# Inverting the 16x16 diagonal blocks on GpSimd ahead of TensorE's levels in the delta-rule inverse

## The reference, cut to what matters

```python
A = jnp.where(strict, jnp.einsum('nbhid,nbhjd->nbhij', kb, k) * decay, 0.0)
M = A + jnp.eye(L, dtype=A.dtype)
u = lax.linalg.triangular_solve(M, v * beta[..., None], left_side=True, lower=True, unit_diagonal=True)
w = lax.linalg.triangular_solve(M, kb * jnp.exp(G)[..., None], left_side=True, lower=True, unit_diagonal=True)
...
def step(S, inp):
    q_i, w_i, u_i, k_i, a_i, gl_i = inp
    v_new = u_i - jnp.einsum('bhld,bhde->bhle', w_i, S)
    o = jnp.einsum('bhld,bhde->bhle', q_i, S) + jnp.einsum('bhls,bhse->bhle', a_i, v_new)
```

## Time and profile before

| what | us |
|---|---|
| median of three runs | 1905.28 |
| the profiled execution | 1905.35 |
| its span, first to last instruction | 1903.5 |
| TensorE busy | 1857.1 |
| VectorE busy | 1354.1 |
| ScalarE busy | 959.2 |
| GpSimd busy | 110.8 |
| start to end of the inverse, first layer (L1352 to L1382) | 1035.39 to 1072.15 |
| start to end of the inverse, second layer | 1632.05 to 1668.81 |

### The profile page before, as it was taken

One profiled execution on the slowest core, in us unless ns is written; L12 is line 12 of the kernel. 1 busy time (PEld: TensorE's weight loads), 2 busy tenths in 40 slices (PEclk: granted clock), 3 DMA queues, 4 the chain that ended last, 5 costly groups with the idle time before them and its releaser, 6 DMA issues.

```text
span 1903.5 us, 31636 instructions
## 1 busy us (share of the span) xinstructions
PE 1857.1 (98%) x12720; PEld 1705.4 (90%) x12720; DVE 1354.1 (71%) x2154; ACT 959.2 (50%) x1429; POOL 110.8 (6%) x112
## 2 busy tenths in 40 slices
PE   8999999999999999999999999999999999999998
PEld 6888999888899989998988989998999888989997
DVE  5576788747677886777777777677766776875545
ACT  5666444656644454435655353435443665454343
POOL 0000000000000000000002201100110001400100
PEclk9999999999999999999999999999999999999999
DMA  7225777531477768774530267775785442036552
GB/s 289 80 77 212 280 280 274 202 105 68 179 271 280 268 236 313 279 269 179 185 124 25 99 228 281 288 281 217 292 303 204 146 147 87 2 133 210 188 207 80
DMA packets 54510, 374.45 MB, mean 197 GB/s; under 512 B 6016, under 2 KB 6656, under 8 KB 12800
## 3 DMA queue, kind: packets, MB, share of 16 engines
q1 hardware_dynamic: 51808, 362.34, 52.0%
q0 software_dynamic: 2304, 9.93, 1.4%
q10 hardware_dynamic: 288, 0.65, 0.1%
HBM read 371.84 MB, written 1.05 MB: 196 GB/s over the span
## 4 chain that ended last, share of the span: by engine, by line
PE 87%; DVE 7%; ACT 4%; issue 1%; DMA 0%; SPq 0%; DVEq 0%; ACTq 0%
PE bank L709 14%; PE bank L711 14%; PE bank L710 14%; PE bank L872 6%; PE bank L873 6%; PE bank L874 6%; PE bank L785 3%; PE bank L786 3%; PE bank L787 3%; PE bank L1352 2%; DVE w_lo L1992 2%; PE bank L1362 1%; PE bank L835 1%; ACT w_hi L1450 1%; PE bank L836 1%
## 5 line engine op out<-in xcount | busy, mean ns | idle before, releaser
L1992 DVE TENSOR_TENSOR w_lo<-raw,w_hi 128x2048 fp32r<-128x2048 f32 (+4 forms) x279 | 608.1, 2183 | 76.4 <-ACT w_hi L1450 76.0
L709 PE MATMUL bank<-hT_hi,w_hi 128*128 128x256 f32 x2304 | 654.1, 284 | 2.0 <-DVE scratch L2751 2.0
L710 PE MATMUL bank<-hT_lo,w_hi 128*128 128x256 f32 x2304 | 651.8, 283 | 0.0
L711 PE MATMUL bank<-hT_hi,w_lo 128*128 128x256 f32 x2304 | 651.8, 283 | 0.0
L1450 ACT ACTIVATE w_hi<-raw 128x2048 fp32r<-128x2048 f32 (+4 forms) x268 | 502.2, 1875 | 147.9 <-PE bank L874 116.2
L709 PEld LDWEIGHTS bank<-hT_hi,w_hi 128*128 128x128 f32 x2304 | 440.1, 191 | 8.9 <-issue 6.5
L710 PEld LDWEIGHTS bank<-hT_lo,w_hi 128*128 128x128 f32 x2304 | 440.2, 191 | 2.8 <-issue 0.5
L711 PEld LDWEIGHTS bank<-hT_hi,w_lo 128*128 128x128 f32 x2304 | 440.2, 191 | 0.2
L872 PE MATMUL bank<-w_hi,hid_hi 128*128 128x512 f32 x528 | 206.7, 392 | 1.2 <-DVE hid_lo L2068 0.8
L873 PE MATMUL bank<-w_lo,hid_hi 128*128 128x512 f32 x528 | 206.2, 391 | 0.0
L874 PE MATMUL bank<-w_hi,hid_lo 128*128 128x512 f32 x528 | 205.4, 389 | 0.0
(11 more groups left out here) (410 smaller groups left out, 2405.5 us busy)
## 6 DMA issues: line engine op xcount, KB each, us to landing
raw<-in_wb SPq DMA_DIRECT2D x158, 1024.0 KB, 4.8
raw<-in_wa SPq DMA_DIRECT2D x94, 1024.0 KB, 4.9
scratch<-in_wm SPq DMA_DIRECT2D x72, 1024.0 KB, 7.0
raw<-in_wb SPq DMA_DIRECT2D x8, 940.0 KB, 4.6
raw<-in_wb SPq DMA_DIRECT2D x4, 936.0 KB, 4.6
lnw<-in_ln_g POOLq DMA_DIRECT2D x6, 512.0 KB, 5.2
lnw<-in_ln_b POOLq DMA_DIRECT2D x6, 512.0 KB, 6.2
scratch<-in_c SPq DMA_DIRECT2D x5, 512.0 KB, 3.6
```

The source lines that it names most:

```text
L709: nc.tensor.matmul(out, ah, bh, start=(i == 0), stop=False)
L710: nc.tensor.matmul(out, ah, bl, start=False, stop=False)
L711: last = nc.tensor.matmul(out, al, bh, start=False, stop=(i == n - 1))
L1992: return nc.vector.tensor_tensor(w_lo[:, slot, cols], raw[:, raw_slot, cols], w_hi[:, slot, cols].bitcast(F32), ALU.subtract)
```

## The change

The levels 0 to 3, blocks of 1, 2, 4 and 8 rows that grow to 16, leave TensorE and VectorE. In their place, in each layer:

1. SyncE writes the two systems of each head to HBM (`system_out`), six DMAs, each of which waits for `dmul` of that head. They stand behind the loads of the last input chunk and of the first three output chunks in SyncE's queue.
2. One DMA (`small_blocks`) gathers the 96 diagonal blocks of 16x16 into `sm`, one block on each of 96 partitions: 16 rows of 64 bytes a partition.
3. GpSimd clears `xx` and the target, and inverts the 96 blocks (`small_inverses`): a negation, a copy, then for blocks of 2, 4 and 8 two products each, every product written out as elementwise multiplications and additions by halves; at the end a transposed copy. Each step waits for the one before (`follow`).
4. One DMA writes both sides of the inverses to HBM, and sixteen DMAs (8 blocks, 2 sides) write them into the diagonal of `xx`, in pieces of 64 bytes.
5. TensorE waits for those sixteen DMAs (`solved_back`) where it waited for `xt`, and does the levels 4 to 6: `NZ` is 9, `CLOSED` is 3. GpSimd's masks (L618) stand behind its inversion.
6. VectorE's `mlstm_norm` steps are moved up to fit nine groups; ScalarE's Sigmoid stands ahead of the loop, the Sqrt behind it.

`first_matrices` is gone. Some semaphores of the first block are merged (`by_pe`, `by_act`); the waits and their order are the same.

```diff
+        def system_out(sp, l, h):
+            sp.wait_ge(B["dmul"], due(B, "dmul", h + 1))
+            sp.dma_start(sys_dram[2 * h:2 * h + 2, 0:P * P].rearrange("k (p n) -> p k n", n=P),
+                         sysT[:, h, :].rearrange("p (k n) -> p k n", n=P)[:, 0:3:2, :]).then_inc(sys_out, 16)
+        def small_blocks(sp, l):
+            sp.wait_ge(sys_out, (l + 1) * GDN_H * 16)
+            sp.wait_ge(lo_done, l * B_N + S_A + B_S0["wout"] + 1 + NEW)
+            sp.dma_start(sm[:, SM_SYS:SM_SYS + SMALL * SMALL].rearrange("q (i j) -> q i j", j=SMALL),
+                         sys_dram.rearrange("u (b n) -> (u b) n", b=NBLK)[:, 0:SMALL * P].rearrange("q (i c) -> q i c", c=P)[:, :, 0:SMALL]
+                         ).then_inc(small_in_place, 16)
+            sp.wait_ge(B["solved"], due(B, "solved", 1))
+            sp.dma_start(inv_dram, sm[:, SM_INVT:SM_INVT + 2 * SMALL * SMALL]).then_inc(solved_out, 16)
+            sp.wait_ge(solved_out, (l + 1) * 16)
+            for b in range(NBLK):
+                rows = slice(b * SMALL, (b + 1) * SMALL)
+                for side in range(2):
+                    sp.dma_start(xx[rows, :, side, rows],
+                                 inv_dram.rearrange("(u b) (s a c) -> b s a u c", b=NBLK, s=2, a=SMALL)[b, side]).then_inc(solved_back, 16)
...
                     load_b(sp, l, n, b_width(n))
+                    h = n - (B_S0["wout"] - 1)
+                    if 0 <= h < 4:
+                        system_out(sp, l, h)
+                    if h == 3:
+                        system_out(sp, l, 4)
+                        system_out(sp, l, 5)
+                        small_blocks(sp, l)
...
+            def product(out, left, right, s):
+                n = SMALL // (2 * s)
+                full = sm[:, SM_PROD:SM_PROD + n * s * s * s].rearrange("q (k b i j) -> q k b i j", k=s, b=n, i=s)
+                for b in range(n):
+                    a = left[:, b].rearrange("q i k -> q k i").unsqueeze(3).to_broadcast([NSMALL, s, s, s])
+                    w = right[:, b].unsqueeze(2).to_broadcast([NSMALL, s, s, s])
+                    last = nc.gpsimd.tensor_tensor(full[:, :, b], a, w, ALU.mult)
+                follow(last)
+                k = s
+                while k > 2:
+                    k //= 2
+                    half = n * s * s * k
+                    follow(nc.gpsimd.tensor_tensor(sm[:, SM_PROD:SM_PROD + half], sm[:, SM_PROD:SM_PROD + half],
+                                                   sm[:, SM_PROD + half:SM_PROD + 2 * half], ALU.add))
+                follow(nc.gpsimd.tensor_tensor(out, full[:, 0], full[:, 1], ALU.add))
+            follow(nc.gpsimd.tensor_scalar(all_sys, all_sys, -1.0, None, ALU.mult))
+            follow(nc.gpsimd.tensor_copy(blocks(SM_INV, 1, 0, 1), blocks(SM_SYS, 1, 0, 1)))
+            for level in range(1, SMALL_LEVELS):
+                s = 1 << level
+                n = SMALL // (2 * s)
+                t = sm[:, SM_T:SM_T + n * s * s].rearrange("q (b i j) -> q b i j", b=n, i=s)
+                product(t, blocks(SM_SYS, s, 0, 1), blocks(SM_INV, s, 1, 1), s)
+                product(blocks(SM_INV, s, 0, 1), blocks(SM_INV, s, 0, 0), t, s)
+            nc.gpsimd.tensor_copy(square(SM_INVT), square(SM_INV).rearrange("q a c -> q c a")).then_inc(B["solved"], 1)
...
         def pool_levels(pool, l):
+            pool.wait_ge(B["fm"], due(B, "fm", N_FEAT))
+            pool.wait_ge(B["zero"], due(B, "zero", 3))
+            nc.gpsimd.memset(xx, 0.0).then_inc(B["clear"], 1)
...
+            pool.wait_ge(small_in_place, (l + 1) * 16)
+            small_inverses(pool)
...
-                level = const(f"lev{n // 3 + 1}").unsqueeze(1).unsqueeze(1).to_broadcast([P, 2, 2, P])
+                level = const(f"lev{n // 3 + SMALL_LEVELS}").unsqueeze(1).unsqueeze(1).to_broadcast([P, 2, 2, P])
...
-                pe.wait_ge(B["xt"], due(B, "xt", len(FIRST)))
+                pe.wait_ge(solved_back, (l + 1) * 2 * NBLK * 16)
```

More of the change, by code:

```diff
@@ L448, in build @@
         LEVELS = P.bit_length() - 1
-        NZ = (LEVELS - 1) * 3
+        SMALL = 16
+        SMALL_LEVELS = SMALL.bit_length() - 1
+        NZ = (LEVELS - SMALL_LEVELS) * 3
         CLOSED = NZ - 6
         V_CHUNK = max(c for c, (f, _, _) in enumerate(B_WIN) if F_LQ - 1 in f)
-        FIRST = [(h, 1) for h in range(GDN_H - 2)] + [(GDN_H - 2, 2)]
+        NSYS, NBLK = 2 * GDN_H, P // SMALL
+        NSMALL = NSYS * NBLK
         B_LAGP, B_LAGT, B_LAGO, B_LAGV = 1, 2, 3, 4
@@ L607, in _, with small_inverses, follow, blocks @@
             sp.wait_ge(out_st, TT * 16)
-        def pool_levels(pool, l):
+        pool_steps = {"n": 0}
+        def small_inverses(pool):
+            def follow(ins):
+                pool_steps["n"] += 1
+                ins.then_inc(B["pl"], 1)
+                pool.wait_ge(B["pl"], pool_steps["n"])
+            def blocks(at, s, row, col):
+                first = at + row * SMALL * s + col * s
+                n = SMALL // (2 * s)
+                v = sm[:, first:first + n * 2 * s * (SMALL + 1)] if n > 1 else sm[:, first:first + SMALL * s]
+                v = v.rearrange("q (b m) -> q b m", b=n)[:, :, 0:SMALL * s]
+                return v.rearrange("q b (i c) -> q b i c", c=SMALL)[:, :, :, 0:s]
+            def product(out, left, right, s):
[13 more added lines that the diff above has]
+                follow(nc.gpsimd.tensor_tensor(out, full[:, 0], full[:, 1], ALU.add))
+            all_sys = sm[:, SM_SYS:SM_SYS + SMALL * SMALL]
+            follow(nc.gpsimd.tensor_scalar(all_sys, all_sys, -1.0, None, ALU.mult))
+            follow(nc.gpsimd.tensor_copy(blocks(SM_INV, 1, 0, 1), blocks(SM_SYS, 1, 0, 1)))
+            for level in range(1, SMALL_LEVELS):
+                s = 1 << level
+                n = SMALL // (2 * s)
+                t = sm[:, SM_T:SM_T + n * s * s].rearrange("q (b i j) -> q b i j", b=n, i=s)
+                product(t, blocks(SM_SYS, s, 0, 1), blocks(SM_INV, s, 1, 1), s)
+                product(blocks(SM_INV, s, 0, 1), blocks(SM_INV, s, 0, 0), t, s)
+            square = lambda at: sm[:, at:at + SMALL * SMALL].rearrange("q (a c) -> q a c", c=SMALL)
+            nc.gpsimd.tensor_copy(square(SM_INVT), square(SM_INV).rearrange("q a c -> q c a")).then_inc(B["solved"], 1)
@@ new lines, in pool_levels @@
+        def pool_levels(pool, l):
+            pool.wait_ge(B["fm"], due(B, "fm", N_FEAT))
+            pool.wait_ge(B["zero"], due(B, "zero", 3))
+            nc.gpsimd.memset(xx, 0.0).then_inc(B["clear"], 1)
+            pool.wait_ge(lo_done, l * B_N + S_A + B_S0["wout"] + 1 + NEW)
+            nc.gpsimd.memset(sm[:, SM_INVT:SM_INVT + 2 * SMALL * SMALL], 0.0).then_inc(B["clear"], 1)
+            pool.wait_ge(B["clear"], due(B, "clear", 2))
+            nc.gpsimd.memset(sm[:, SM_INV:SM_INV + (SMALL + 1) * SMALL].rearrange("q (i n) -> q i n", n=SMALL + 1)[:, :, 0:1], 1.0
+                             ).then_inc(B["clear"], 1)
+            pool.wait_ge(B["clear"], due(B, "clear", 3))
+            pool.wait_ge(small_in_place, (l + 1) * 16)
+            small_inverses(pool)
+            pool.wait_ge(B["solved"], due(B, "solved", 1))
@@ L1080, in compressed @@
                                                         start=True, stop=True)
-                        last.then_inc(A["cs"], 1)
+                        last.then_inc(A["by_pe"], 1)
                     if step == CPT_AT:
@@ L1095, in compressed @@
                                                     start=True, stop=True)
-                        last.then_inc(A["co"], 1)
+                        last.then_inc(A["by_pe"], 1)
                 pe.wait_ge(A["pj"], due(A, "pj", A_WIN))
@@ L2813, in _ @@
                         outputs_b(step - B_LAGV)
-                    if 0 <= step - MOBA_H + 1 < 3:
-                        first_matrices(len(FIRST) - 1, step - MOBA_H + 1)
                     if step == NUB:
```

109 lines of the change are left out of this document (48 added, 61 removed), and 1 row of the table B.

## The result

The kernel after takes 1892.45 us (median of four runs, 1892.02 to 1893.44) where the kernel before took 1905.24 beside it (1905.10 to 1905.32). The ratio is 0.9934, with a 95% interval of 0.9922 to 0.9946. The forecast was 1910.1, and its sign was wrong. The rival "the chain fits" had been worked out at 1893.

A forecast was written before the change was run, and what follows sets the result against it. TensorE, busy 98%, was taken as the bound; a 37.6 us chain from 1013.25 plus a 23.7 us inverse put the first user at 1074.55 against 1072.15, so 1905.3 + 4.8 = 1910.1 us, range 1888 to 1938.

The forecast's parts named there:

- the chain fits: Rival: short waits and small transfers lie near their lower bounds, chain 29.0 us, kernel faster at 1893; chance 0.33.
- The saving: Three levels of three groups leave TensorE's inverse, 5.48 us each, 16.44 us a layer.
- the remaining stretch: Shorter inverse, TensorE's start to first user: 20.32 us plus 1.5 and 1.9, together 23.7 us.
- two surcharges: Added to the shorter inverse: 1.5 us for VectorE's slip in its first level, 1.9 us for a lower clock at its opening.
- The turning point: Chain length, last system's end to TensorE's start, at which the change neither wins nor loses: 35.2 us.
- 1, last systems out: Chain's start: the last head's systems written to HBM, 128 KB, taken as 2.3 us.
- link 3: GpSimd's inversion in the chain: 29 instructions and 20 waits at 0.30 us, 15.2 us by rows, taken as 17.
- link 2: Gather of 96 KB in 1536 pieces of 64 bytes, between 2.1 and 12.3 us, taken as 5.5.
- 4, inverses out: Inverses written to HBM after GpSimd's inversion, 192 KB in rows of 2 KB, taken as 2.3 us.
- link 5: Sixteen DMAs back, 192 pieces of 64 bytes each, between 7.1 and 22.5 us, taken as 10.
- The dear GpSimd: Rival: GpSimd instructions have a fixed cost of half a microsecond, inversion 27.4 us, chain 48.0, kernel 1931; chance 0.11.
- the dear pieces: Rival: 64-byte pieces cost what 2 KB packets do, gather 12.3 us, return 22.5, chain 56.9, kernel 1949; chance 0.07.

The follow-up runs named there:

- Experiment 9: Kernel after with all normalization steps ahead of the inverse's first subtraction and 34 unread identity transposes on TensorE in the wait; 1885.97 us, ratio 0.9901 to the kernel before.
- experiment 3: Kernel after with the last product of GpSimd's inversion done three times, for a longer chain; 1905.7 us, ratio 1.0003 to the kernel before.
- Experiment 4: Kernel after with 20 more dependent 96x8 copies on GpSimd in the chain; 1904.42 us, ratio 0.9996 to the kernel before.
- Experiment 5: Kernel after with two return DMAs into a compact buffer instead of sixteen, VectorE placing blocks by six masked multiplications; 1894.85 us, ratio 0.9943 to the kernel before.
- Experiment 7: Kernel after with the sixteen return DMAs split, eight issued from ScalarE's queue and eight from SyncE's; 1885.64 us, ratio 0.9899 to the kernel before.
- experiment 2: Kernel after without the chain: no gather, GpSimd inversion or return, TensorE working on cleared blocks, a bound only; 1879.41 us, ratio 0.9864 to the kernel before.
- experiment 6: Kernel after with two return DMAs, placing shared by GpSimd and VectorE, weight split's last quarters ahead, 12 transposes in the wait; 1893.41 us, ratio 0.9940 to the kernel before.
- experiment 11: Kernel after with returns on two queues, three normalization steps ahead of the subtractions and 16 transposes in the wait; 1881.91 us, ratio 0.9877 to the kernel before.

## Why the prediction was wrong

**What was right.** The saving was 16.44 a layer and the remaining stretch 23.7: measured 23.47 (1042.12 to 1065.59). Its two surcharges were 1.5 for VectorE's slip and 1.9 for the clock. The six last groups took 15.75 where two levels and the way to the first user had been 14.84 (20.32 less 5.48; 14.69 by their own starts, 1057.46 to 1072.15), so the slip is 0.9 to 1.1, and the clock cost 2.2. The slip came the way it was forecast: the gaps that end at 1051.41 and 1054.63 each end 0.1 behind a transpose of the first level that normalization step 1 or 2 had delayed. Experiment 9 takes both away and comes to 20.10. That the chain would be late and would decide was right too: TensorE stood still for 6.53 us before its start. The turning point was put at 35.2. Experiments 3 and 4, with chains of 35.73 and 35.01 and first users 0.14 and 0.54 before the old place, put it at 35.9 and 35.5 in the profiled executions.

**The step that failed is the sum of the links**, 37.6 predicted and 29.03 measured:

| link | predicted | measured | read from, to |
|---|---|---|---|
| 1, last systems out | 2.3 | 1.84 | 1013.09, 1014.93 |
| 2, gather | 5.5 | 2.73 | 1014.93, 1017.66 |
| 3, GpSimd | 17 | 12.52 | 1017.66, 1030.18 |
| 4, inverses out | 2.3 | 2.77 | 1030.18, 1032.95 |
| 5, sixteen back | 10 | 9.17 | 1032.95, 1042.12 |
| hand-offs | 0.5 | in the above | |

Two links hold 7.3 of the 8.6 us. With either of them right the forecast's chain would have been under its turning point of 35.2 (33.1 with link 3, 34.8 with link 2), and the sign with it.

*Link 3*, the term that was most mis-sized. The prediction priced a `follow` at 0.30, from the one row in which GpSimd waited for itself, where a DMA issue stood behind a product. Between two elementwise steps the trace has 0.08 (0.20 from 1018.57, next start 1018.85), the bound below in the prediction's own text. Over 20 waits that is 1.6 in place of 6.0, 4.4 too much. The instructions themselves take 12.52 - 1.6 = 10.9 where the formula gave 9.2, since a small one with two inputs takes 0.20 (96x8) where it gives 0.13; and the 1.8 put on for four-dimensional patterns were not needed, as the 96x512 product takes 1.155, less than the 1.27 of a plain 128x512. So -4.4, +1.7 and -1.8 make the -4.5. Experiment 4 measures the step by itself. The Trainium skill's rates (GPSIMD Engine Reference, performance versus the Vector engine) had made link 3 an estimated 17.4, with the same price for the waits; the trace has 12.52 and disagrees with the estimate, mostly by the waits.

*Link 2.* The gather of 1536 pieces landed in 2.5 us, near the 2.1 of the bound below and 10 from the bound above. The price of a packet of 2 KB was kept in part, and there is next to no such price here. Experiment 5 shows the same from the other side: two DMAs of 1536 pieces, issued one right behind the other, land 3.3 us after their issue. The Trainium skill (DMA: Bandwidth & Descriptors, Specifications) warns of pieces below 512 bytes. At this size, 96 KB, the traces show at most 0.4 us of it for one DMA (2.5 against 2.1 in the earlier trace rows) and at most 1.2 for each of two under way together (3.3).

*Link 5* was nearly right, and for the reason that the prediction counted against the rival: the issues follow each other. An issue takes 0.47 where the bound below had 0.33, and one landing of 1.6 stands behind the last. Experiment 7 shows that it is the queue.

**The rivals.** "The chain fits" had 3.5, 13, 7.5 and twice 2.25 for its links and 29.0 for the sum. The sum was met to 0.03 and the time to 0.6 us, but in parts by errors that offset each other: link 5 was 1.7 longer, links 2 and 3 together 1.3 shorter. The dear GpSimd (27.4) and the dear pieces (56.9 for the chain) are excluded by the rows above. So the rival's mechanism ran for the waits and the gather and not for the sixteen returns, and that its time was met so closely is luck in part. The prediction knew of both cheap values: of 10.8, 15.2 and 27.4 for link 3 it took the middle one and then added to it, where the 0.08 between VectorE and GpSimd already spoke for the cheap wait.

**What stays open.** Why the clock falls in the window from 1036 in after and only in that from 1037 in the run with the longer chain is not settled, nor why a filling in the second layer of experiment 9 ran at full speed (34 transposes in 3.93 us, and the clock stayed at 1.00 through the 1.95 us of idle time behind them) and in the first not (5.60). How much of the loss in experiments 2, 5 and 6 is VectorE's lateness and how much the clock that fell behind it was not separated. And a version in which both VectorE's and GpSimd's work around the start is thinned out was not tried; by experiment 2 this work, and not the chain, is the bound near 1879.

## What to carry to other kernels

When work moves off the critical engine onto a chain of small steps, find the turning point first, then ask which links the forecast's sign hangs on, and price a hand-off by a row of the same pair of operations, not by the one row that happens to wait. For a burst of small DMAs count issues and not bytes: a second queue was worth 3.4 us a layer, where fewer DMAs with a spreading step on a busy engine were worth nothing. A wait put into TensorE's list cost again at its end here, by the lower clock (2.2 us a layer), and the filling that outlasted the wait gave nothing where the shorter ones gave something. And where a row names an engine whose work was long done, look at the end of every other input: in experiments 2, 6 and 11 it was VectorE and not GpSimd.

## What the runs showed of the hardware

- A small GpSimd step that waits for the one before it costs 0.25 to 0.26 us in all (20 in 5.05, 96x8), of which 0.08 or less is the wait.
- 1536 pieces of 64 bytes land in 2.5 us in one DMA, and with two such DMAs under way in 3.3 each. An issue of 192 pieces occupies its queue for 0.47 to 0.50 us, one of 1536 for 0.33 (the gather) or 0.57 (experiment 5), and two queues issue side by side.
- VectorE and GpSimd slow each other down when both run products of tiles in SBUF. VectorE's 128x512 product goes from 0.69 to 1.75 us and its 768-wide one from 0.95 to 2.0; GpSimd's 128x512 product goes from 1.27 to between 1.6 and 2.0. It need not hit both: in experiment 5 VectorE's took 1.77 and GpSimd's beside it 1.27. VectorE's subtraction, which reads one operand from a bank, was not slowed (0.69 or less at 1055.40 in after, beside a mask of 1.27).
- By the means of the 1 us windows (an estimate), the granted clock fell to 0.50 some 0.9 us into the idle time at the end of the attention units in after, in both layers, and some 2.4 us into it in experiment 3. TensorE had been busy 0.27 and 0.59 of the last two us of the first layer's units in after. With transposes of the identity from 1036.3 on it fell all the same in that layer; it was back in the window from 1039 (56 of them) or 1040 (34, 16), and without any in that from 1046 in after and from 1042 where TensorE started at 1039.29 (experiment 7). In the second layer of experiment 9, with 34 of them, it did not fall. It also fell behind waits of 1.1 to 2.7 us inside the inverse (experiments 2, 5 and 6, first layer).
